# The norm behind the down projection, the next input projection and the final stores move into the layer's block, in two token halves

## The reference, cut to what matters

```python
xn = rmsnorm(h, norm_g[layer, 0])
mix = mixer_even(xn, ...) if layer % 2 == 0 else mixer_odd(xn, ...)   # begins with xn @ w_in, ends with @ w_out
h = h + rmsnorm(mix, norm_g[layer, 1])
ff = swiglu(rmsnorm(h, norm_g[layer, 2]), ffn_wg[layer], ffn_wu[layer], ffn_wd[layer])
h = h + rmsnorm(ff, norm_g[layer, 3])
```

## Time and profile before

| | us |
|---|---|
| median of 3 runs | 1893.98 (1892.92 to 1895.62) |
| the profiled execution, its own time | 1898.12 |
| its span, from the first to the last instruction | 1896.6 |
| layer 0: from the last down product to the first product of the odd input projection | 1054.1 to 1086.4 |
| layer 0: odd input projection on PE | 1086.4 to 1236.2 |
| layer 1: from the last down product to the first transpose of y | 1859.2 to 1885.3 |
| layer 1: transposes, copies and stores of y to the end of the span | 1885.3 to 1896.6 |

### The profile page before, as it was taken

The page is one execution under the profiler, slowest core; times in us unless marked ns, Lnnn a source line. Parts: engine busy times, 40 slices in busy tenths (PEclk is TensorE's granted clock), DMA queues, the critical chain, the costliest instruction groups (busy, mean ns, idle before and its releaser), DMA issues. The chain is left out here.

```text
span 1896.6 us, 31249 instructions
## 1 busy us (share of the span) xinstructions
PE 1711.6 (90%) x12427; PEld 1553.7 (82%) x12427; DVE 829.7 (44%) x1503; ACT 450.5 (24%) x656; POOL 292.4 (15%) x368
## 2 busy tenths in 40 slices
PE   5999998698887999999999899979579999999995
PEld 4999954465547899999999599956278999999994
DVE  3332544534434753444322633357657543443225
ACT  4111311122213522222111311132334222221111
POOL 1411001001000043333100000030200433331000
PEclk9999987677988999999999999988679999999998
DMA  4222210142874123333332022230131233333311
GB/s 129 89 71 78 67 49 1 51 145 83 273 235 144 34 67 88 88 88 83 106 91 64 33 68 88 88 87 1 50 108 29 67 88 88 88 91 98 91 30 47
DMA packets 225248, 159.70 MB, mean 84 GB/s; under 512 B 18041, under 2 KB 206437, under 8 KB 225048
## 3 DMA queue, kind: packets, MB, share of 16 engines
q1 hardware_dynamic: 220832, 156.40, 28.2%
q0 software_dynamic: 3280, 1.85, 0.5%
q10 hardware_dynamic: 1064, 0.51, 0.1%
HBM read 149.11 MB, written 9.88 MB: 84 GB/s over the span
## 5 line engine op out<-in xcount | busy, mean ns | idle before, releaser
L1883 PE MATMUL psum<-mixed_high,w_high 128*128 128x280 f32 x1472 | 310.5, 292 | 20.7 <-DVE mixed_low L2109 18.7
L1883 PE MATMUL psum<-mixed_high,w_low 128*128 128x280 f32 x1472 | 312.4, 294 | 0.0
L1883 PE MATMUL psum<-mixed_low,w_high 128*128 128x280 f32 x1472 | 309.6, 292 | 0.0
L1994 ACT CAST w_high<-ring 128x1024 fp32r<-128x1024 f32 (+1 forms) x128 | 144.5, 1129 | 659.1 <-PE psum L1883 630.7
L2101 DVE TENSOR_TENSOR w_low<-ring,w_high 128x1024 fp32r<-128x1024 f32 (+1 forms) x128 | 212.7, 1662 | 141.8 <-ACT w_high L1994 141.8
L1883 PEld LDWEIGHTS psum<-mixed_high,w_high 128*128 128x128 f32 x1472 | 235.9, 190 | 21.9 <-DVE w_low L2101 19.6
L1883 PEld LDWEIGHTS psum<-mixed_high,w_low 128*128 128x128 f32 x1472 | 236.4, 190 | 0.0
L1883 PEld LDWEIGHTS psum<-mixed_low,w_high 128*128 128x128 f32 x1472 | 233.9, 189 | 0.0
L348 PE MATMUL psum<-normed_high,w_high 128*128 128x280 f32 x832 | 174.9, 292 | 3.8 <-PEq L531 3.8
L348 PE MATMUL psum<-normed_high,w_low 128*128 128x280 f32 x832 | 176.4, 293 | 0.0
L348 PE MATMUL psum<-normed_low,w_high 128*128 128x280 f32 x832 | 174.5, 291 | 0.0
(11 more groups left out here) (400 smaller groups left out, 2822.3 us busy)
## 6 DMA issues: line engine op xcount, KB each, us to landing
ring<-in_ffn_wd SPq DMA_DIRECT2D x16, 1408.0 KB, 7.0
ring<-in_ffn_wg SPq DMA_DIRECT2D x40, 512.0 KB, 3.9
ring<-in_ffn_wu SPq DMA_DIRECT2D x40, 512.0 KB, 5.1
projected<-in_cache_fox_k SPq DMA_DIRECT2D x64, 256.0 KB, 4.1
ring<-in_w_in_even SPq DMA_DIRECT2D x14, 1024.0 KB, 5.3
ring<-in_w_in_odd SPq DMA_DIRECT2D x12, 1024.0 KB, 5.0
v_pages<-in_cache_fox_v SPq DMA_DIRECT2D x32, 256.0 KB, 3.5
projected<-in_cache_fox_v SPq DMA_DIRECT2D x16, 256.0 KB, 3.1
```

Source lines behind the costliest of these rows:

```text
L1883: done = mm(banks[2 * tl + a][:, 0:HALF], w, m[a], start=first and s == 0, stop=last and s == 2)
L1994: nc.scalar.copy(dst, src).then_inc(w_hi[p], 1)
```

## The change

The norm behind the down projection, and what follows it, move into the block of `close_layer`.

- The last down tile (tile 7) is made in two token halves by `down_piece`: half a over both pieces, then half b. PE waits for both pieces before half a. After five chunks of half b, `sum_first_half` puts the column sums of half a's squares in between.
- ACT squares each down tile as soon as it is copied out, DVE adds the squares up (`acc_o`, `sq_o`), in the course of the down projection. POOL has no part in the norm any more; the `warm` products are gone.
- The post-norm, residual sum and pre-norm are the two functions `normalise` on ACT and DVE, which were the code behind the out projection, now called a second time with other buffers. `first_tiles` on PE is the same for the products.
- Layer 0: ACT and DVE split the first four odd input tiles into `g_h`, `g_l` before DVE's `normalise`; the first four tiles follow the normalised chunks, the other 20 run in a loop as before, with the same engines for splitting and copying out. SP sends the units of `w_in_odd` and then of `w_out_odd` from this block. `close_sems()` comes after the input projection.
- Layer 1: `normalise` without a pre-norm; the 12 turning jobs use 4 banks instead of 8, a job starts when its half of `h` is done, DVE's six copies stand behind all of DVE's `normalise`. `close_sems()` comes after the stores.

```diff
+        last_layer = layer == 1
+        if not last_layer:
+            proj = place(right, "projected", [128, 7 * 4 * T], side="right")
+            Pt = proj[:, :].rearrange("p (k t) -> p k t", k=28)
...
+        n_h, n_l = at("normed_high_a", 11792, [128, KC, HALF], F32R), at("normed_low_a", 14032, [128, KC, HALF], F32R)
+        n_b = at("normed_b", 16272, [128, KC, 2, HALF], F32R)
+        acc_o, sq_o = at("ffn_square_sum", 39232, [128, T]), at("ffn_squares", 39792, [128, T])
+        g_h, g_l = at("next_w_high", 0, [128, 4, 1024], F32R), at("next_w_low", 20752, [128, 4, 1024], F32R)
+        sq_n = [at("next_squares", col, [128, HALF]) for col in (*range(4096, 6056, HALF), 24848)]
+        acc_n = at("next_square_sum", 25128, [128, T])
+        yt = at("tokens_out", 0, [128, 6, D])
...
                 for slot in range(2):
                     when_split(31 + slot)
-                    if units[1] is not None:
-                        send(sp, units[1], slot, slot)
+                    send(sp, units[1], slot, slot)
...
+                for slot in range(2):
+                    sp.wait_ge(next_lo, 2 * slot + 2)
+                    send(sp, units[1], slot, 2 + slot)
+                with sp.Fori(0, 4) as i:
+                    for slot in range(2):
+                        when_split(i * 2 + (33 + slot))
+                        send(sp, units[1], slot, i * 2 + (4 + slot))
+                for slot in range(2):
+                    when_split(41 + slot)
+                    send(sp, units[2], slot, slot)
...
+                def down_piece(m, slot, p, halves, between=None):
+                    wh, wl = chunks(w_h[:, p, :], 11), chunks(w_l[:, p, :], 11)
+                    for k in range(11):
+                        kk = 11 * p + k
+                        if len(halves) == 2:
+                            last = both(2 * slot, wh[:, k], wl[:, k], [t[:, kk, :] for t in hid_h],
+                                        [t[:, kk, :] for t in hid_l], kk == 0, kk == FC - 1)
+                        else:
+                            a = halves[0]
+                            last = one(banks[4 * slot + a], wh[:, k], wl[:, k], hid_h[a][:, kk, :], hid_l[a][:, kk, :],
+                                       kk == 0, kk == FC - 1)
+                        if between is not None and k == 4:
+                            between()
+                    return last
...
+                        down_tile(i, slot)
+                down_tile(3, 0)
+                for p in range(2):
+                    pe.wait_ge(w_lo[p], 32)
+                pe.wait_ge(tile_evac[2], 14)
+                down_piece(7, 1, 0, (0,))
+                down_piece(7, 1, 1, (0,)).then_inc(f_half, 1)
+
+                def sum_first_half():
+                    pe.wait_ge(tile_evac[0], 15)
+                    pe.wait_ge(f_acc, 6)
+                    mm(banks[1][:, 0:HALF], ones[:, :], acc_o[:, HALVES[0]], start=True, stop=False)
+                    pe.wait_ge(f_sq, 8)
+                    mm(banks[1][:, 0:HALF], ones[:, :], sq_o[:, HALVES[0]], start=False, stop=True).then_inc(o_sum, 1)
+
+                down_piece(7, 1, 0, (1,), sum_first_half).then_inc(used[0], 1)
+                down_piece(7, 1, 1, (1,)).then_inc(used[1], 1)
+                if last_layer:
+                    pe.wait_ge(f_sq, 9)
+                    for i, src in enumerate((acc_o, sq_o)):
+                        last = mm(banks[3][:, 0:HALF], ones[:, :], src[:, HALVES[1]], start=(i == 0), stop=(i == 1))
+                    last.then_inc(o_sum, 1)
+                    for j, (b, kk) in enumerate(Y_JOBS):
+                        t0, n = BLK[b]
+                        pe.wait_ge(h_done, 16 + KC * (t0 + n > HALF) + kk + 4)
+                        if j >= 4:
+                            pe.wait_ge(y_copied[j % 2], (j - 4) // 2 + 1)
...
+                            pe.wait_ge(o_evac_b, 3)
+                        for i in range(4):
+                            last = mm(banks[4 + j % 4][0:n, i * 128:(i + 1) * 128], h[:, kk + i, t0:t0 + n], ident[:, :],
+                                      start=True, stop=True, is_transpose=True)
+                        last.then_inc(y_turned[j % 2], 1)
+                    return
+                first_tiles(1, g_h, g_l, lambda a, k: (n_b[:, k, 0], n_b[:, k, 1]) if a else (n_h[:, k], n_l[:, k]),
+                            (acc_o, sq_o), (f_sq, 9), acc_n)
+                with pe.Fori(1, 6) as i:
...
-                def down_turn(i, slot):
+                nc.scalar.activation(eps[:, 1:2], eps[:, 0:1], ACT.Sqrt)
+
+                def down_turn(i, slot, first=False):
                     for p in range(2):
...
                         act.wait_ge(used[p], i * 2 + (27 + slot))
                         high(w_h[:, p, :], down_raw(1 - slot, p), p)
...
+                    act.wait_ge(tile_evac[2 * slot], i + 12)
+                    if not first:
+                        act.wait_ge(f_acc, i * 2 + (slot - 1))
+                    o_ = out[:, bass.ds(i * 2 + slot, 1), :].rearrange("p a t -> p (a t)")
+                    nc.scalar.activation(acc_o[:, :] if first else sq_o[:, :], o_, ACT.Square).then_inc(f_sq, 1)
...
                 down_turn(3, 0)
+                act.wait_ge(f_evac, 1)
+                act.wait_ge(f_acc, 6)
+                nc.scalar.activation(sq_o[:, HALVES[0]], out[:, 7, HALVES[0]], ACT.Square).then_inc(f_sq, 1)
...
+                    raw = ring[:, t // 2, 0:2048].rearrange("p (k a n) -> p k a n", k=KC, a=2)[:, :, t % 2]
+                    nc.scalar.copy(chunks(g_h[:, t, :]), raw).then_inc(next_hi, 1)
+
+                if not last_layer:
+                    next_first(0)
+                o_root_of(1, 0)
+                if not last_layer:
+                    for t in range(1, 4):
+                        next_first(t)
+                act.wait_ge(used[1], DOWN_END)
+                nc.scalar.activation(sq_o[:, HALVES[1]], banks[5][:, 0:HALF], ACT.Square).then_inc(f_sq, 1)
+                nc.scalar.copy(out[:, 7, HALVES[1]], banks[5][:, 0:HALF]).then_inc(o_evac_b, 1)
+                if last_layer:
+                    o_root_of(1, 1)
+                    for j in range(1, len(Y_JOBS), 2):
+                        b, kk = Y_JOBS[j]
...
+                def in_high(i, q):
+                    p = q % 2
...
+                    if not first:
+                        dve.wait_ge(f_sq, i * 2 + (slot + 1))
+                        if not (isinstance(i, int) and i == 0):
+                            dve.wait_ge(f_acc, i * 2 + (slot - 1))
+                        v.tensor_tensor(acc_o[:, :], acc_o[:, :], sq_o[:, :], ALU.add).then_inc(f_acc, 1)
...
+                down_turn(3, 0)
+                dve.wait_ge(f_half, 1)
+                v.tensor_copy(out[:, 7, HALVES[0]], banks[4][:, 0:HALF]).then_inc(f_evac, 1)
+                if last_layer:
+                    normalise(1, out, (layer, 3), None, None, None, None)
+                    for j in range(0, len(Y_JOBS), 2):
+                        b, kk = Y_JOBS[j]
+                        dve.wait_ge(y_turned[0], j // 2 + 1)
+                        n = BLK[b][1]
+                        v.tensor_copy(yt[0:n, b, kk * 128:(kk + 4) * 128], banks[4 + j % 4][0:n, :]).then_inc(y_copied[0], 1)
+                    return
+
+                def in_raw(slot, p):
+                    return ring[:, slot, 0:2048].rearrange("p (k a n) -> p k a n", k=KC, a=2)[:, :, p]
+
+                def in_low(slot, p, count):
+                    low(chunks(w_l[:, p, 0:1024]), in_raw(slot, p), chunks(w_h[:, p, 0:1024]), p, count)
...
+                    dve.wait_ge(next_hi, t + 1)
+                    v.tensor_tensor(chunks(g_l[:, t, :]), in_raw(t // 2, t % 2), chunks(g_h[:, t, :]).bitcast(F32),
+                                    ALU.subtract).then_inc(next_lo, 1)
+                normalise(1, out, (layer, 3), (layer + 1, 0),
+                          lambda a, k: (n_b[:, k, 0], n_b[:, k, 1]) if a else (n_h[:, k], n_l[:, k]),
+                          lambda a, k: sq_n[k][:, :], acc_n)
+                in_low(0, 0, 33)
+                for a in range(2):
+                    dve.wait_ge(h_root, 2 + a + 1)
+                    v.reciprocal(rstd[:, HALVES[a]], rstd[:, HALVES[a]])
+                v.drain()
+
...
+                def in_evac(i, q):
+                    dve.wait_ge(used[q % 2], i * 2 + (35 + q // 2))
+                    for a in range(2):
+                        o_ = Pt[:, bass.ds(i * 4 + q, 1), HALVES[a]].rearrange("p a t -> p (a t)")
+                        last = v.tensor_tensor(o_, banks[2 * q + a][:, 0:HALF], rstd[:, HALVES[a]], ALU.mult)
...
+                        in_evac(i, q)
+                        in_low(1 - q // 2, q % 2, i * 2 + (32 + q // 2))
+                for q in range(4):
+                    in_evac(5, q)
+                    if q < 2:
+                        in_low(1, q, 42)
 
...
-    close_layer(0, (out_even, odd), True)
+
```

(59 more changed lines are left out.)

260 lines of the change are left out of this document (141 added, 119 removed).

## The result

| | before | changed |
|---|---|---|
| median of the runs, us | 1894.80 (4 runs, 1892.92 to 1896.77) | 1874.73 (4 runs, 1870.98 to 1879.85) |
| profiled execution: own time, span | 1898.12, 1896.6 | 1876.49, 1874.0 |
| mean granted clock of TensorE | 0.926 | 0.922 |

The ratio is 0.9896, with a 95% interval of 0.9868 to 0.9923. The change gains 20.1 us by the medians and 22.6 us by the spans of the two profiles. The forecast was 25.9 us, so the kernel is faster, by less than forecast; the median lies at the upper edge of the range (1861 to 1875).

A forecast was written before the change was run, and what follows sets the result against it. PE is busy 90% of the span, so time can come only from stretches without model products. Layer 0's 16.3 us plus layer 1's 9.6 make 25.9, from 1893.98 to 1868 us; range 1861 to 1875, over 0.85.

The forecast's parts named there:

- Tile 7: Last down tile, both layers: PE stands 3.1 us for both pieces, and a clock fall adds 1.7 us.
- Half a's sum and root: Last down tile: the root of half a's summed squares is ready 16.8 us after the end of down tile 6.
- Splits ahead of the reciprocal: Layer 0, DVE: splitting four odd tiles delays the reciprocal to 21.5 us after down tile 6, giving away 4.7 us.
- First product and fifth tile: Layer 0 input projection: first product at 25.4 us, a clock fall behind its 2.5-us wait, fifth tile at 58.8 us.
- The 20 tiles: Rest of layer 0's input projection: pitch 6.16 us, 123.2 us in all, last product at 182.0 us.
- Rival 3: Layer 0 input projection: late splits make PE wait per tile, giving the gain back; 1898 us at 1.5 us, chance 0.03.
- rival 4: Both layers: DVE's chain, not its placement, sets the time; nothing gained, 1894 us, chance 0.03.
- The barrier: Block end, moved behind the input projection in layer 0 and the stores in layer 1: 0.8 us added each.
- Layer 1: Behind down tile 6: last copy at 40.6 us, gain 10.4 us, 0.8 more for the barrier, so 9.6 us.
- rival 1: Clock holds at the waits in tile 7 and before the norm: gain 30.8 us, 1863 us, chance 0.2.
- Rival 2: Low clock follows every wait, also the 2.0-us one between halves and pauses around the fourth tile: 1873 us, chance 0.13.
- the sum's bound of the clock: Sum of both layers: none of the three clock falls gives 1863 us, two further ones 1871 us.

The follow-up runs named there:

- wait_filled: Changed kernel plus three products of ones on PE before its wait for both pieces of the last down tile: 1869.09 us.
- tail_act: On top of piece_wait, ScalarE copies all of the first four turning jobs in layer 1, DVE only from the fifth: 1858.42 us.
- late_twice: Changed kernel plus a drain and VectorE's four products of qs, done twice more at the end of the rotation: 1865.38 us.
- piece_wait: Changed kernel, but PE waits for piece 1 of the last down tile only before using it: 1857.06 us.
- after_again: The changed kernel run and profiled once more, unaltered: 1875.12 us, ratio 0.9886.
- recip_first: On top of piece_wait, DVE's reciprocal of half a goes between the first and second of the four low parts: 1856.35 us.

## Why the prediction was right in the changed stages and wrong in what it left out

- **Tile 7.** Wait forecast 3.1 us, measured 3.16 in both layers. The fall that comes with it was priced at 1.7 us and cost about 2.7: half a took 1048.54 - 1037.24 = 11.3 us instead of 8.5. PE made products at 0.50 from 1037.24 to 1042.8. Over the 12 waits of 3.16 us in seven profiles half a took 11.3 to 11.6 us seven times, 10.2 or 10.3 three times and 8.8, at the full clock, twice. A fall is thus worth 2.5 to 2.8, 1.5 or 0 us beside the 8.8. Which of them it is goes with the moment at which the granted clock falls in the trace: 1.9 to 2.5 us into the wait in the seven costliest cases, 2.9 us into it or 0.4 and 1.1 us behind its end in the three of 1.5.
- **Half a's sum and root.** Forecast 16.8, measured 17.8 (1051.92): the extra microsecond of the fall.
- **Splits ahead of the reciprocal.** Forecast reciprocal 21.5, measured 22.2 (1056.30). Given away 4.4 us, forecast 4.7. Putting it first brought 2.45 us with the clock's part, not 4.4: three low parts (3.4 us) then stand between the reciprocal and the norm, and these the same first products need.
- **First product and fifth tile.** Forecast 25.4 and 58.8, measured 26.1 and 59.3. The wait was 2.21 us (forecast 2.5). A low clock followed it in six of the nine profiles that have it. It cost 1.4 us up to the fifth tile (forecast 1.5), and 3.0 in the two profiles (`wait_filled`, `tail_act`) in which the wait between the halves brought another.
- **The 20 tiles** kept their pitch: clock 1.00 over the 117 us, last product at 183.1 (forecast 182.0, before 199.2). Rival 3 falls, and so does rival 4: PE stood 2.2 us ahead of the first odd tile instead of 32.3.
- **The barrier** of layer 0 went from 1.17 to 1.88 us, 0.7 for 0.8. Layer 0: 15.4 of 16.3 us.
- **Layer 1.** Last copy at 1870.87, so 41.7 against 40.6, the extra microsecond of the fall again, but the end behind it took 3.1 us instead of 3.4, not the 0.8 more. So 9.6 of 9.6 us is luck: two misses of 1.1 us that cancel.
- **The clock rivals.** In the profile shown rival 1 (it holds) fails at tile 7 in both layers and ahead of the first odd tile. Rival 2 (every wait) fails there too: the 1.97-us wait between the halves (1077.13) was followed by 1.00. Its mechanism is real all the same: in three of the eleven profiles that have this wait (`wait_filled`, `tail_act`, `late_twice`) the low clock came with it and cost 1.5 us. The case in the section of the Trainium skill quoted with it, "TensorE: Matmul & The Clock Gate", "HAM oscillation — how this bites in real kernels", has waits of some 3 to 5 us; the step to every wait of 2 us was the prediction's own. So was its rule by length ("clearly over 2 us"), which its own rows spoke against: a fall behind 1.97 us and none around 2.94. The length of a wait alone doesn't tell.

**The step that failed** is the sum's bound of the clock: "the three clock falls, none of them (4.9 less, 1863) or two further ones". It counted falls in the changed stretches alone and so took every other stage at the length it had, a term of 0 us. The state stage measured +6.1 us (+5.7 in the repeat), by a granted clock of 0.60 instead of 0.81 over its last part. In the profile the 25.9 of the forecast are 24.9 in the changed stages, minus 6.1, plus 2.9 at the start of the kernel, plus 0.9 in the rest: 22.6. The 2.9 us lie in the decode stages, which the change doesn't touch; the same stretch varied from 578.5 to 583.9 us over the profiles, so I give it no cause. With the loss taken away by a small shift, the kernel took 1866.27 and 1865.38 us, beside the forecast of 1868.

**What stays open.** The level goes with the place of the first fall in the stage, over 14 profiles; only the two delayed kernels moved that place on purpose and changed the level. Why the clock falls at these moments, and why a fall 0.15 us later into the stage (21.66 in `piece_wait`, 21.51 in `after_again`) is worth 5.6 us, isn't shown. It isn't the rotation's length: 20.66 us of it occurred with 89.2 (`after_again`) and with 80.9 (`recip_first`). It is also not wholly fixed by the program: of nine executions of the changed kernel one was under 1870 us (1867.33), and of eight with the delay one was over it (1872.76). So the level could be read back from the traces but not foretold, and the long low clock was avoided, not explained.

## What to carry to other kernels

A stage that the change doesn't touch can change its length through TensorE's clock. When a time misses the sum, cut both traces at the same instructions and compare stages, before doubting the terms of the changed part; then shift the stage's start by half a microsecond, to see whether its time hangs on the placement. When a product loop is rearranged into halves, let each wait stand right ahead of the first product that needs it: one wait put 33 products too early cost 5.9 and 6.1 us in the two layers here, beside 15.4 and 9.6 us that the whole rearrangement gained. Small edits that show in their stage (2.45 and 1.05 us) don't show in medians that scatter by 4 us and more, so read them in the profile.

## What the runs showed of the hardware that was not expected

- The same stage, with the same instructions, takes 81, 83.5 or 89.3 us, by the stretches of it that PE spends at granted 0.50, and these go with the place of the first fall in it (21.4 to 21.5 us into the stage: 89; 21.1 or 21.7: 81.5 and 83.6). In the longest case PE stayed at 0.50 for some 16 us though it was busy 3.03 to 4.00 of every 4 us.
- The same wait has different consequences. With 3.16 us the low clock cost 2.5 to 2.8 us (seven times), 1.5 (three) or nothing (two); with 2.2 us it came in six profiles of nine, with 1.97 us between the halves in three of eleven. Two falls of the kernel before were read as 1.7 us each.
- Three products of ones in a wait of 3.16 us kept the clock at 1.00 and saved 2.2 to 2.9 us of layer 1's tail, though the wait for the data stayed.
